# Gate one-hots of a PEER layer: the gate multiply of every second group moves from GpSimd to ScalarE

## The reference, cut to what matters

```python
idx = e1 * PEER_NKEYS + e2                      # 128 x 128 experts
gate = jax.nn.softmax(best, axis=-1)
...
act = jax.nn.gelu(einsum('phkd,pd->phk', u_tab[ib], tb)) * gb
out = einsum('phk,phkd->pd', act, v_tab[ib])
```

## Time and profile before

| what | us |
|---|---|
| median of three runs (3575.87 to 3579.18) | 3577.81 |
| the profiled execution's own time | 3578.59 |
| its span, first to last instruction | 3576.7 |
| TensorE busy | 3462.9 (97%) |
| VectorE busy | 2373.3 (66%) |
| ScalarE busy | 1548.0 (43%) |
| GpSimd busy | 941.5 (26%) |

### The profile page before, as it was taken

The page is one execution under the profiler, slowest core; times in us unless marked ns, Lnnn a source line. Parts: engine busy times, 40 slices in busy tenths (PEclk is TensorE's granted clock), DMA queues, the critical chain, the costliest instruction groups (busy, mean ns, idle before and its releaser), DMA issues.

```text
span 3576.7 us, 55854 instructions
## 1 busy us (share of the span) xinstructions
PE 3462.9 (97%) x22489; PEld 3167.0 (89%) x22489; DVE 2373.3 (66%) x3955; ACT 1548.0 (43%) x2424; POOL 941.5 (26%) x705
## 2 busy tenths in 40 slices
PE   8999999999899999999999999999999999999998
PEld 8988999999797778788767887899999998999998
DVE  7435465545744646555477553549998997898997
ACT  7254443222635444322358353334336664333333
POOL 4010023111401002311111400115544565344441
PEclk9999999999999999999999999999999999999999
DMA  4211232222121123322222022336766998999995
GB/s 151 67 52 60 77 124 83 94 90 89 65 77 55 64 77 124 100 94 95 100 71 77 31 95 71 106 104 232 241 215 226 326 328 297 354 364 365 368 367 198
DMA packets 191825, 552.34 MB, mean 154 GB/s; under 512 B 20176, under 2 KB 69456, under 8 KB 191184
## 3 DMA queue, kind: packets, MB, share of 16 engines
q1 hardware_dynamic: 130080, 376.51, 30.6%
q0 software_dynamic: 36864, 134.23, 10.8%
q10 hardware_dynamic: 24624, 38.01, 2.9%
HBM read 504.64 MB, written 44.04 MB: 153 GB/s over the span
## 4 chain that ended last, share of the span: by engine, by line
PE 75%; DVE 16%; ACT 3%; DMA 3%; issue 1%; POOL 1%; ACTq 0%; DVEq 0%; POOLq 0%
PE PSM L316 16%; PE PSM L317 16%; PE PSM L318 16%; PE PSM L210 5%; PE PSM L3173 5%; PE PSM L3174 5%; PE PSM L3175 5%; DVE PARTS L283 3%; DMA CH<-peer_rows_dram,MQ 2%; DVE MQ L3404 2%; DVE CH L3421 2%; DVE MQ L3400 1%; ACT PARTS L274 1%; PE PSM L1060 1%; DVE MH L1740 1%
## 5 line engine op out<-in xcount | busy, mean ns | idle before, releaser
L274 ACT ACTIVATE PARTS<-RAW 128x1024 fp32r<-128x1024 f32 x612 | 645.6, 1057 | 898.5 <-PE PSM L318 482.9
L316 PE MATMUL PSM<-UX,PARTS 128*128 128x264 f32 (+3 forms) x2912 | 974.5, 335 | 28.7 <-DVE UX L2296 4.9
L317 PE MATMUL PSM<-UX,PARTS 128*128 128x264 f32 (+3 forms) x2912 | 957.6, 329 | 0.0
L318 PE MATMUL PSM<-UX,PARTS 128*128 128x264 f32 (+3 forms) x2912 | 957.1, 329 | 0.0
L283 DVE TENSOR_TENSOR PARTS<-RAW,PARTS 128x1024 fp32r<-128x1024 f32 (+1 forms) x612 | 746.5, 1225 | 305.6 <-ACT PARTS L274 305.4
L316 PEld LDWEIGHTS PSM<-UX,PARTS 128*128 128x128 f32 x2912 | 550.6, 189 | 80.0 <-issue 12.3
L317 PEld LDWEIGHTS PSM<-UX,PARTS 128*128 128x128 f32 x2912 | 551.0, 189 | 29.6 <-issue 1.7
L318 PEld LDWEIGHTS PSM<-UX,PARTS 128*128 128x128 f32 x2912 | 549.7, 189 | 29.8
L3173 PE MATMUL PSM<-AC,PARTS 128*128 128x384 f32 x1024 | 343.6, 336 | 5.4 <-DVE AC L3469 5.4
L3174 PE MATMUL PSM<-AC,PARTS 128*128 128x384 f32 x1024 | 342.7, 335 | 0.0
L3175 PE MATMUL PSM<-AC,PARTS 128*128 128x384 f32 x1024 | 342.7, 335 | 0.0
(11 more groups left out here) (506 smaller groups left out, 6032.5 us busy)
## 6 DMA issues: line engine op xcount, KB each, us to landing
RAW<-w_ff_dram SPq DMA_DIRECT2D x128, 512.0 KB, 3.2
RAW<-peer_u_dram SPq DMA_DIRECT2D x128, 512.0 KB, 4.5
RAW<-peer_v_dram SPq DMA_DIRECT2D x128, 512.0 KB, 6.3
RAW<-w_in_dram SPq DMA_DIRECT2D x116, 512.0 KB, 3.3
acts_dram<-MQ ACTq DMA_DIRECT2D x128, 192.0 KB, 4.0
MQ<-acts_dram SPq DMA_DIRECT2D x128, 192.0 KB, 6.3
RAW<-w_mix_o_dram SPq DMA_DIRECT2D x32, 512.0 KB, 3.3
MQ<-gates_dram SPq DMA_DIRECT2D x32, 512.0 KB, 7.9
```

The costliest lines, as they stand in the source:

```text
L274: e.activation(p[:, 0:1024], self.raw.of(i), ACT.Copy).then_inc(S.sem, S.tick("w", i))
L316: e.matmul(dst, wh[k], xh_[k][:, lo:hi], start=(k == 0), stop=False, skip_group_check=True)
L317: e.matmul(dst, wh[k], xl_[k][:, lo:hi], start=False, stop=False, skip_group_check=True)
L318: m = e.matmul(dst, wl[k], xh_[k][:, lo:hi], start=False, stop=(k == kk - 1), skip_group_check=True)
```

## The change

GpSimd no longer multiplies. ScalarE's one Relu of `1 - x` over four tokens becomes four, each with the token's own numbers: `Relu(gate - gate * x)`, which is the gate where x is 0 and zero elsewhere, by `bias=Gt[:, t]` and `scale=` the negated gate. `onA` of the second group so has the gate in it, and `onB` stays a plain one-hot. The negated gates come from one more ScalarE copy per block of 128 tokens (three in all), from the PSUM transpose that already yields the gates; they lie in columns of `Y` that the stage did not use. TensorE no longer waits for GpSimd.

```diff
+        Gn = [x[:, TD:T2] for x in Y[0:3]]
...
# peer_pe, gates
                     if half:
                         e.wait_ge(S.sem, S.at("onA", i4))
-                        e.wait_ge(G.sem, G.at("onB", i4))
...
# peer_act, one_hots
-                e.activation(a, a, ACT.Relu, bias=con["ones"][:, 0:1], scale=-1.0).then_inc(S.sem, S.tick("onA", i4))
+                g, u0 = Gn[FILLS[n][0]], t0 - 128 * FILLS[n][0]
+                for i in range(4):
+                    e.activation(a[:, 128 * i:128 * i + 128], a[:, 128 * i:128 * i + 128], ACT.Relu, bias=Gt[:, t0 + i:t0 + i + 1],
+                                 scale=g[:, u0 + i:u0 + i + 1]).then_inc(S.sem, S.tick("onA", i4))
...
# peer_act, where a block's e1, e2 and gates leave PSUM
                     e.wait_ge(T.sem, T.at("e12", n))
+                    e.activation(Gn[n], PSM[:, ps.of("e12", n), 256:384], ACT.Copy, scale=-1.0).then_inc(S.sem, S.tick("minus", n))
...
# peer_pool
-            def one_hots(n, t8):
-                i4 = four_at(n, t8) + 1
-                t0 = FILLS[n][1] + 8 * t8 + 4
-                o = onB[i4 % 4].rearrange("p (t n) -> p t n", t=4)
-                e.wait_ge(V.sem, V.at("onB", i4 - 1))
-                e.tensor_tensor(o, o, Gt[:, t0:t0 + 4].unsqueeze(2).to_broadcast([128, 4, 128]), MUL).then_inc(
-                    G.sem, G.tick("onB", i4))
...
-                for n, t8 in gates_at(i + 1):
-                    one_hots(n, t8)
```

## The result

The changed kernel took **3547.2 us** (median of 4 runs, 3545.92 to 3550.24), beside 3576.84 for the kernel before (4 runs, 3575.73 to 3579.18). The ratio is 0.9918, 95% interval 0.9900 to 0.9935: 29.6 us faster, where 16.5 was forecast. The sign and the mechanism came out as forecast; the forecast size is little more than half of the measured one, and the time lies under the range. The profiled execution took 3545.92 us, with a span of 3544.1.

A forecast was written before the change was run, and what follows sets the result against it. VectorE, stalled by GpSimd's multiply, was taken to bound the gates' stage. 12.25 us from the stage, 3.4 from the step to pd and 0.8 from the clock made 16.5: 3578.6 to 3562.1, median 3561 us, range 3556 to 3574.

The forecast's parts named there:

- The bound and the mechanism: Gates' stage: VectorE is the bound, its group of four (L3404) losing 0.72 or 1.46 us while GpSimd multiplies.
- The stage's 14.25 us: TensorE's time lost in 29 late tiles of the gates' stage, at 6.44 us each instead of 5.95.
- VectorE's sum: VectorE's work in the gates' stage: 15.65 us per three tiles, 19.3 with stalls, or 6.43 a tile.
- The gather ring, 2 us: Gates' stage: VectorE waits 2.75 us per three tiles for rows in three gather buffers; 2 us of the gain lost.
- the prediction's sign for the ring: Sign of being wrong: gathers landing at 9 us or more, with VectorE's waits for them over 20 us in total.
- The stage's after-effects, 0.8 us for the clock: Around the step from pu to pd: shorter idle keeps the clock at 2.4 GHz; from 0 to 1.9 us, 0.8 taken.
- The step, 3.4 us: From pu's last matmul to the pd loop: idle of 4.12 us falls to 0.7, saving 3.4 if VectorE is ahead.
- ScalarE, nothing: Gates' stage: four Relus add 0.8 to 1.2 us a tile, hidden in ScalarE's 1.67 wait for TensorE; cost none.
- The ring as the bound (3571): Rival, gates' stage: rows land 1 us later (9.0), a cycle of three tiles stays 19.4 us; 3571 us, chance 0.17.
- No effect (3578): Rival, gates' stage: the stall is the gather's or VectorE's own, so L3404 stays 1.8 to 2.6; 3578 us, chance 0.08.
- The slower case, gathers held up by the group: Rival, gates' stage: VectorE's L3404 group delays gathers' descriptors, rows land up to 2.2 us later; 3588 us, chance 0.07.
- The prediction's comparison of 1.71 with 1.72: Against the slower rival: a gather beside the L3404 group took 1.71 us, one without it 1.72.

The follow-up runs named there:

- no_multiply: The kernel before without GpSimd's multiply and TensorE's wait for it, nothing in its place: 3553.63 us, ratio 0.9933.
- ones_on_pool: The changed kernel with GpSimd's multiply put back, by a column of ones, and TensorE waiting for it: 3577.3 us, ratio 1.0004.
- dve_4more: The changed kernel with VectorE's group of four made twice per tile, GpSimd without a multiply: 3578.53 us, ratio 1.0005.
- b_again: The kernel before, unchanged, timed and traced a second time: 3577.58 us, ratio 0.9997.
- here_27: The changed kernel with three of the thirty early dots moved into the gates' stage: 3549.3 us, ratio 0.9922.
- abs_twice: The changed kernel with ScalarE's four Abs made twice, 1.3 us more a tile: 3572.25 us, ratio 0.9992.
- pool_late: The kernel before, with GpSimd's multiply waiting until VectorE's group of four ends: 3568.6 us, ratio 0.9978.
- later_start: The changed kernel with the gates' stage begun one tile later (all six fills moved): 3549.25 us, ratio 0.9929.

## Why the prediction was right or wrong

**The bound and the mechanism: right.** VectorE set the stage's pace by being held in its group of four while GpSimd multiplied. Taking the multiply away gives it all back (no_multiply), putting it back as an empty multiply takes it all (ones_on_pool), and 1.1 us of VectorE work do the same as the stalls (dve_4more). The stage's 14.25 us, read from TensorE's three gates, measured 14.4 between the two profiles and 16.1 against b_again. That VectorE's sum came to 6.43, beside TensorE's 6.44, was in part luck. In the 29 late tiles of before 16 groups take 1.83 and 13 take 2.57, so the stalls are 3.15 us per three tiles and not 3.64; in their place stand 0.4 us of waits for rows (4.1 us in those tiles), which the sum left out.

**The gather ring, 2 us: mis-sized; it cost nothing.** The prediction's rows land in 8.0 us and would make VectorE wait 2.75 per three tiles. They land in 7.8 and it waited 25.0 us in 40 tiles, 1.9 per three. What it can spare is 17.85 - 15.65 = 2.2 per three, so no wait reached TensorE. Half of the prediction's sign for the ring, waits over 20 us in total, did show, without gathers at 9 us or more; it was badly chosen: 40 tiles x 2.2 / 3 = 29 us of spare time must turn up as waits of some kind (25.0 + 3.1 did). Only a wait of TensorE counts. here_27 shows that the worry was in place: with three more dots the ring does reach TensorE.

**The stage's after-effects, 0.8 us for the clock: the step that failed most.** Two sizes were missed, by asking only when pd starts and not how pu ends and pd goes on. Pd's first five tiles fell from 24.32 to 20.88 us, 3.4. 1.6 of it is the clock, by the starts of the first 16 matmuls in before and after: in before's totals by stretch, TensorE ran at a granted 0.60 right behind the idle of 4.12, at the 1.2 GHz level for most of 4.3 us, and at 1.00 after that:

```profile
3024.68:3029.00 4.32, 4.32 (x16) 4.32 (x17) 4.13 (x8) 2.00 (x3) 3.41 (x4) 0.60 0.94 319
3029.00:3049.00 20.00, 18.68 (x107) 18.10 (x105) 8.83 (x16) 6.00 (x8) 1.80 (x2) 1.00 0.96 358
```

(1 - 0.60) x 4.32 is 1.7 us, nearly the same. The prediction read this, at 1.9, but took less than half of it; behind the 0.89 idle of after the granted clock stayed at 1.00. The other 1.8 is that VectorE was still late for two of the next tiles, 0.76 and 0.56 us of idle with a slower start behind each, which the prediction left out though the rows stand in before's timeline:

```profile
3039.75 0.41 PE L3173 MATMUL PSM<-AC,PARTS 128*128 128x384 f32 x1 [0.76 <-DVE AC L3469]
...
3044.74 0.41 PE L3173 MATMUL PSM<-AC,PARTS 128*128 128x384 f32 x1 [0.56 <-DVE AC L3469]
```

And the end of pu, which the prediction moved as it was, went from 27.95 (30.16 in b_again) to 26.91, because VectorE was late with the low halves of pu's weights (L283) too: TensorE waits 0.76 us for them in before, 2.7 in b_again and not at all in after. In before's timeline:

```profile
3016.13 0.41 PE L316 MATMUL PSM<-UX,PARTS 128*128 128x384 f32 x1 [0.76 <-DVE PARTS L283]
```

**The step, 3.4 us: right**, 3.2 measured (2.7 against b_again).

**ScalarE, nothing: right but for 0.4 us in the first tile.** Relus of 0.48, 0.74 us of idle left, inside the forecast 0.5 to 0.9, and abs_twice shows what it costs when the cover is gone.

**The sum.** With the mean of the two traces of before against after: stage 15.25 where 12.25 was taken (2 of it the ring), first tile 0.8 and end of pu 2.1 where nothing was taken, step 3.0 for 3.4, pd's start 3.5 for 0.8. Together 24.6 for 16.5. From 3578.6, the profiled time of before, that is 3554, and without the 1.2 us of the first tile's clock 3555: even the effect alone lies under the low end of 3556. The further 5 us come from ahead of the stage, and that they are the change's isn't shown.

**The rivals.** The ring as the bound (3571): not here, but near. No effect (3578): excluded. The slower case, gathers held up by the group: not seen. The eight gathers that run into a group in this stretch take 1.98, but what held them is the instruction ahead of the group (last section), and the group beside them keeps its 1.11. The prediction's comparison of 1.71 with 1.72 came to the right end by the wrong reading: both had been held, by other instructions. pool_late shows what such a change of sides looks like: the stall goes to the next instruction of VectorE, and the time stays within 0.3% of before.

## What to carry to other kernels

When an engine has been the bound for a while, what it fell behind by can be paid again at the next boundary: in the idle there, in the clock behind that idle, and in the first tiles after it. So it was with VectorE here, and not with ScalarE (abs_twice). Sum those from the trace as terms of their own, up to the point where the bounding engine has caught up. And moving an instruction that holds another engine in time can merely choose whom it holds, as in pool_late; giving it to an engine with idle time, one that doesn't meet VectorE, removes it.

## What the runs showed of the hardware

GpSimd's multiply of 128x512 and VectorE hold each other in both orders: the group of four takes 1.83 or 2.57 us instead of 1.11, L283 2.05 instead of 1.21, and the multiply itself 2.04 instead of 1.06. A gather's issue on GpSimd is held too, by VectorE instructions of two operands from memory that are already running. VectorE and GpSimd in after's timeline:

```profile
2732.35 1.22 DVE L283 TENSOR_TENSOR PARTS<-RAW,PARTS 128x1024 fp32r<-128x1024 f32 x1
2732.70 1.68 POOL L3508 DMA_INDIRECT CH<-peer_rows_dram,MQ  x1 [2.13 <-DVE CH L3425]
...
2739.07 1.22 DVE L3404 TENSOR_TENSOR MQ<-MH,MQ 128x1024 f32<-128x1024 f32 x1
2739.13 1.98 POOL L3508 DMA_INDIRECT CH<-peer_rows_dram,MQ  x1 [0.30 <-issue]
2740.21 1.11 DVE L3408 TENSOR_SCALAR MQ<-MH,MQ 128x128 f32<-128x128 f32 x4
...
2748.31 0.94 POOL L3508 DMA_INDIRECT CH<-peer_rows_dram,MQ  x1 [3.90 <-DVE CH L3425]
```

The first ends at 2734.38, 0.81 after the end of L283 (2733.57); the second at 2741.11, 0.82 after that of L3404 (2740.29), with the group of four beside it for most of that time, and neither held by the other; the third meets nothing and takes 0.94. Of the 68 gathers between 2731 and 2970, 50 start beside such an instruction and end 0.80 to 0.82 after it, and the 18 others, three of which start in its last 0.03 us, take 0.93 or 0.94. A gather that is under way does not hold VectorE's next one: L3404 keeps its 1.22 behind the first. Before had this as well (1.93, 1.72 and 1.71 in the earlier trace rows), so the change neither brought nor cured it.

The same instructions ahead of the stage brought TensorE to its first gates anywhere between 2687.40 and 2698.61 us in these traces, 11 us of 3580, though the times from there on repeat to 1 us. The kernels with GpSimd's multiply (four traces) and those without it (five; later_start and here_27 have other work ahead of the stage) average 2695.1 and 2692.3, a difference that so few traces with this spread don't establish. The delay builds up in small steps and no row names its cause; it stays open. For a change of 10 us in such a kernel, counting from a mark in the trace just ahead of the change tells more than the total.
